# Phase copies with consecutive blocks for the key compression of a decoder step

## What is computed

```
def compress(k, pe, w1, w2):
    n_cmp = (k.shape[1] - CMP_BLOCK) // CMP_STRIDE + 1
    idx = jnp.arange(n_cmp)[:, None] * CMP_STRIDE + jnp.arange(CMP_BLOCK)[None, :]
    kb = k[:, idx] + pe[:, None, :]
    hid = jax.nn.silu(jnp.einsum("bclgd,ldh->bcgh", kb, w1))
    ...
    return jnp.einsum("bcgh,hd->bcgd", hid, w2), c_end
```

## Time and profile before

| | |
|---|---|
| median of three runs | 1095.35 us (1095.02 to 1096.1) |
| the profiled execution's own time | 1095.09 us |
| its span in the trace | 1092.9 us |
| PE busy | 1023.7 us, 94% of the span |
| DVE / ACT / POOL busy | 639.7 / 404.9 / 380.9 us |
| share of PE in the chain that ended last | 85% |
| first layer of the compression | from 588.62 to 665.22 us of the span |

### The profile page before, as it was taken

The page is one execution under the profiler, slowest core; times in us unless marked ns, Lnnn a source line. Parts: engine busy times, 40 slices in busy tenths (PEclk is TensorE's granted clock), DMA queues, the critical chain, the costliest instruction groups (busy, mean ns, idle before and its releaser), DMA issues.

```text
span 1092.9 us, 19375 instructions
## 1 busy us (share of the span) xinstructions
PE 1023.7 (94%) x7232; PEld 846.4 (77%) x7232; DVE 639.7 (59%) x1383; ACT 404.9 (37%) x794; POOL 380.9 (35%) x325
## 2 busy tenths in 40 slices
PE   2999999999999879998999999999789999999996
PEld 0989989989989568997997447999757777756685
DVE  5598998998998686214620001244688888844112
ACT  5333333333342584223311002135467777721001
POOL 2487887887887573010000000000323233200000
PEclk9999999999999879998999999999989999999797
DMA  8334533543541902340570004322260000260002
GB/s 330 94 102 110 169 110 101 155 134 98 137 154 40 317 12 82 109 162 1 198 189 1 1 0 147 112 78 78 78 241 1 0 1 1 96 232 1 1 1 82
DMA packets 43017, 108.02 MB, mean 99 GB/s; under 512 B 20675, under 2 KB 21731, under 8 KB 38531
## 3 DMA queue, kind: packets, MB, share of 16 engines
q1 hardware_dynamic: 42946, 106.99, 29.9%
HBM read 81.87 MB, written 12.17 MB: 86 GB/s over the span
## 4 chain that ended last, share of the span: by engine, by line
PE 85%; DVE 6%; ACT 3%; issue 3%; POOL 3%; DMA 0%; DVEq 0%; ACTq 0%
PE ps L561 49%; PE ps L944 7%; PE ps L721 5%; PE ps L834 5%; PE ps L587 4%; POOL C L1720 3%; PE ps L822 2%; PE ps L719 2%; PE ps L539 1%; PE ps L930 1%; PE ps L811 1%; PE ps L813 1%; DVE KL L1479 1%; PE ps L830 1%; PE ps L786 1%
## 5 line engine op out<-in xcount | busy, mean ns | idle before, releaser
L561 PE MATMUL ps<-Hh,ringAh 128*128 128x256 f32 (+1 forms) x768 | 161.0, 291 | 14.3 <-DVE X L1254 14.3
L561 PE MATMUL ps<-Hh,ringAl 128*128 128x256 f32 (+1 forms) x768 | 159.4, 289 | 0.0
L1298 DVE SCALAR_TENSOR_TENSOR acc<-VP,tapc,acc 128x512 f32<-128x512 f32 x122 | 159.2, 1305 | 0.0
L561 PE MATMUL ps<-Xl,ringAh 128*128 128x256 f32 (+1 forms) x768 | 158.1, 287 | 0.0
L1689 POOL TENSOR_TENSOR ringAl<-ringA,ringAh 128x1024 fp32r<-128x1024 f32 x48 | 121.3, 2541 | 73.2 <-ACT ringAh L1020 73.2
L561 PEld LDWEIGHTS ps<-Hh,ringAh 128*128 128x128 f32 x768 | 123.3, 189 | 27.2 <-DVE X L1254 14.6
L561 PEld LDWEIGHTS ps<-Xl,ringAh 128*128 128x128 f32 x768 | 123.9, 189 | 0.0
L561 PEld LDWEIGHTS ps<-Hh,ringAl 128*128 128x128 f32 x768 | 123.1, 189 | 0.0
L1298 DVE SCALAR_TENSOR_TENSOR ps<-VP,tapc,ps 128x512 f32<-128x512 f32 x138 | 102.8, 745 | 0.6
L834 PE MATMUL ps<-PTB,V 128*128 128x512 f32 (+3 forms) x256 | 91.0, 439 | 2.7 <-ACT PTB L1197 2.3
L561 PE MATMUL ps<-Hh,ringEh 128*128 128x256 f32 (+1 forms) x384 | 82.0, 295 | 7.0 <-DVE ringEl L1364 4.6
(11 more groups left out here) (232 smaller groups left out, 2086.7 us busy)
## 6 DMA issues: line engine op xcount, KB each, us to landing
ringA<-in_w_a SPq DMA_DIRECT2D x16, 1536.0 KB, 7.1
G<-VP SPq DMA_DIRECT2D x60, 260.0 KB, 4.8
ringE<-in_w_f SPq DMA_DIRECT2D x24, 512.0 KB, 3.3
ringC<-in_w_c SPq DMA_DIRECT2D x8, 1024.0 KB, 5.7
cache_cmp<-in_cache_cmp SPq DMA_DIRECT2D x32, 128.0 KB, 2.6
cache_sel<-in_cache_sel SPq DMA_DIRECT2D x16, 256.0 KB, 2.9
cache_win<-in_cache_win SPq DMA_DIRECT2D x1, 4096.0 KB, 13.6
out_win_s<-in_win_state SPq DMA_DIRECT2D x1, 4032.0 KB, 17.0
```

The lines of the kernel that those rows point to most:

```text
L561: mm = nc.tensor.matmul(dst, w, x[:, cols], start=begins, stop=ends)
L1298: nc.vector.scalar_tensor_tensor(tap_sum(k % 2), src, w, tap_sum(k % 2), ALU.mult, ALU.add).then_inc(conv_step, 1)
```

## The change

The key pairs are sorted by phase (pair index modulo 8) into copies on the chip, in which the blocks of one phase lie next to each other. As a block is 16 pairs and blocks are 8 pairs apart, pair 8a+m of block c (a is 0 or 1) is entry c+a of phase m. So PE reads columns a, a+1, a+2, ... of phase m.

- `KKm` [128, 2, 8 phases, 4*32+2] at NR: POOL fills it once, from `KK`, with one copy for each kv as soon as that kv's tiles are kept. Two columns at its end take the positional input of that phase for a=0 and a=1, so that the positional sum becomes column 128 of the same matmul. That matmul has 129 consecutive columns (32 for each group, of which 31 are used).
- `cmpm` [128, 8 phases, 32, 16] at G0: DVE fills it from `cache_cmp`, 16 copies of 128x512, each read with a step of 8 columns. It has room for one kv; the copies for kv=1 wait until PE is done with the same phase of kv=0 (`cmpm_used`). DVE starts after the last token tile (`tok_done` 5), since `wtokh` lies in the same bytes.
- PE issues two matmuls for each weight in place of three (129 columns of `KKm`, 480 columns of `cmpm` as 32 runs of 15), with the weights in the order m, a. It waits for `kkm_ready` once for each kv and for `cmpm_ready` ahead of each phase (16 waits).
- The memsets on POOL move: the pads of `hp` and `hs` lie in the bytes of `KKm`, so they are set after `hid_done` 2; the clearing of `vcd` and `qblk` stands behind them.
- ACT waits for `cmpm_used` 16 in place of `hid_done` 2; DVE's bias copy reads column 128 of banks 0 and 1.

```diff
@@ layout
+        KKm = at("KKm", [P, 2, CSUB, GROUPS * 32 + 2], NR)
+        cmpm = at("cmpm", [P, CSUB, SEQS * GROUPS, 16], G0)
@@ tensor
-            pe.wait_ge(cmp_in, 32 * SEQS * NPG)
             pe.wait_ge(v_kept, 4)
             for kv in range(2):
                 if kv == 1:
                     gate_rows()
-                for m in range(CBLK // 2):
-                    w, first, last = W1[:, kv, m, :], m == 0, m == CBLK // 2 - 1
-                    nc.tensor.matmul(ps[:, kv, 0:GROUPS * NCP], w, KK[:, kv, :, m:m + 8 * (NCP - 1) + 1:8],
-                                     start=first, stop=last)
-                    nc.tensor.matmul(ps[:, 4 + kv, 0:SEQS * GROUPS * NCS], w,
-                                     cache_cmp[:, kv, :, m:m + 8 * (NCS - 1) + 1:8], start=first, stop=last)
-                    mm = nc.tensor.matmul(ps[:, 6 + kv, 0:1], w, pe_in[:, kv, m:m + 1], start=first, stop=last)
-                mm.then_inc(hid_done, 1)
+                pe.wait_ge(kkm_ready, kv + 2)
+                for m in range(CSUB):
+                    pe.wait_ge(cmpm_ready, CSUB * kv + m + 1)
+                    for a in range(2):
+                        w, first, last = W1[:, kv, CSUB * a + m, :], m == a == 0, m == CSUB - 1 and a == 1
+                        mm = nc.tensor.matmul(ps[:, kv, 0:GROUPS * 32 + 1], w, KKm[:, kv, m, a:a + GROUPS * 32 + 1],
+                                              start=first, stop=last)
+                        if last:
+                            mm.then_inc(hid_done, 1)
+                        mm = nc.tensor.matmul(ps[:, 4 + kv, 0:SEQS * GROUPS * NCS], w, cmpm[:, m, :, a:a + NCS],
+                                              start=first, stop=last)
+                    mm.then_inc(cmpm_used, 1)
@@ scalar
-            act.wait_ge(hid_done, 2)
+            act.wait_ge(cmpm_used, 2 * CSUB)
@@ vector, ahead of the gate reduction
+            dve.wait_ge(cmp_in, 32 * SEQS * NPG)
+            dve.wait_ge(tok_done, 5)
+            for i in range(2 * CSUB):
+                kv, m = divmod(i, CSUB)
+                if kv:
+                    dve.wait_ge(cmpm_used, m + 1)
+                nc.vector.tensor_copy(cmpm[:, m], cache_cmp[:, kv, :, m::CSUB]).then_inc(cmpm_ready, 1)
...
-            nc.vector.tensor_copy(pe_hid[:], ps[:, 6:8, 0]).then_inc(pe_kept, 1)
+            nc.vector.tensor_copy(pe_hid[:], ps[:, 0:2, GROUPS * 32]).then_inc(pe_kept, 1)
@@ gpsimd
             pool.wait_ge(h2_ready, KT)
+            pool.wait_ge(small_in, 96)
+            nc.gpsimd.tensor_copy(KKm[:, :, :, GROUPS * 32:], pe_in[:].rearrange("p v (a m) -> p v m a", a=2)).then_inc(kkm_ready, 1)
+            for kv in range(2):
+                pool.wait_ge(kv_kept, 2 * kv + 2)
+                nc.gpsimd.tensor_copy(KKm[:, kv, :, 0:GROUPS * 32].rearrange("p m (g c) -> p m g c", g=GROUPS),
+                                      KK[:, kv].rearrange("p g (c m) -> p m g c", m=CSUB)).then_inc(kkm_ready, 1)
+            pool.wait_ge(hid_done, 2)
             nc.gpsimd.memset(hp[:, :, :, NCP:32], 0.0)
             nc.gpsimd.memset(hs[:].rearrange("p v g (s c) -> p (v g s) c", c=16)[:, :, NCS:16], 0.0).then_inc(pads2_set, 1)
```

More of the change, by code:

```diff
@@ L51 @@
 CSTRIDE, CBLK = 16, 32
+CSUB = CSTRIDE // 2
 NCP = (NP_ - CBLK) // CSTRIDE + 1
@@ L338, in build @@
         gates_ready = sem("gates_ready")
+        cmpm_ready = sem("cmpm_ready")
+        cmpm_used = sem("cmpm_used")
+        kkm_ready = sem("kkm_ready")
         hid_done = sem("hid_done")
@@ L1142, in _ @@
                 nc.scalar.activation(hp[:, kv, :, 0:NCP],
-                                     ps[:, kv, 0:GROUPS * NCP].rearrange("p (g c) -> p g c", g=GROUPS),
+                                     ps[:, kv, 0:GROUPS * 32].rearrange("p (g c) -> p g c", g=GROUPS)[:, :, 0:NCP],
                                      ACT.Silu, bias=pe_hid[:, kv:kv + 1]).then_inc(hid_ready, 1)
```

## The result

The changed kernel takes 0.966 of the time before (interval 0.962 to 0.971). Its four runs were 1056.9, 1058.1, 1066.0 and 1066.5 us (median 1062.05); those of the kernel before, beside it, 1095.0, 1095.4, 1096.1 and 1101.1 (median 1095.7). The profiled execution took 1058.09 us, with a span of 1056.0 against 1092.9. So 37 us are gained in the pair of profiles, where 41.2 were forecast, and the times of one kernel lie up to 10 us apart.

The account below looks back on a forecast made before the run. PE alone was taken to bound the compression stage; 0.96 first copy + 33.9 steps + 0.57 gate rows = 35.4 us against 76.6, so 1095.1 - 41.2 = 1053.9 us, range 1051.3 to 1061.5.

Parts of the forecast that it names:

- What bounds the kernel: Compression stage, 76.6 us: PE is busy throughout and no other engine shares in its end, so shortening it shortens the span.
- Cached keys: Compression stage, 32 matmuls of 480 columns in runs of 15: 0.82 us each, near the pace of consecutive columns, from 1.72.
- The 32 hops: Jumps between runs of 15 columns in each cached-keys matmul: possibly 0.06 us a matmul, 1.9 us in all, allowed in the range.
- New keys: Compression stage, 32 matmuls of 129 consecutive columns for 124 scattered ones: 0.24 us each, between 0.22 and 0.34.
- First copy: DVE's first copy of cached keys, on the path at the stage's start: 0.69 us plus 0.07 signal, PE starting 0.96 after 588.62.
- The worst bound of 1.45: Upper bound in us for DVE's first copy, if the 32-byte step slows DVE by PE's factor of 2.1.
- Other copies, waits, POOL's fill, moved memsets: DVE's other 15 copies, PE's 18 waits, POOL's KKm copies and later memsets: cost nothing; waits at most 0.9 us in all.
- The stage: Compression matmuls from 588.62 to the next tile: 35.4 us against 76.6, with 32 steps of 1.06 us; 41.2 less.
- The clock behind the stage: After the compression stage, dips of the clock can fall otherwise: put at 1 us either way in the range.
- a rival only for the compression stage: Whole compression stage at 1.2 GHz: steps of 2.12 us, time 1087.8; chance 0.02.
- The dip at 631: Grant fall near 631 us in the old compression stage, read as falling among slow matmuls; a dip as long costs about 2 us.
- Rival 3: Behind the stage, the gain is partly given back by a transfer now too late; a third of it gives 1068; chance 0.04.

## Why the prediction was right, and where it was off

- **What bounds the kernel, and that the stage's gain reaches what follows**: right. The stall behind it moved by 41.54 us, unchanged in length, and the first two bursts by 41.4.
- **Cached keys** at 0.82 us, measured 0.80 to 0.81: right, with its reason (a record is 566 ns, not 590). The 32 hops cost nothing (1.9 us had been allowed), and the run with other steps shows that it is the neighbour within 8 bytes that counts. One reading behind it was loose: of the matmul at 632.55 that was named as running at the lower level, only the first 0.8 us did, as the grant is back at 1.00 from 633.34. The one ahead of it lies in the low stretch whole (629.93 to 633.34), and bears the reading out with 1.71 us from start to start:

```profile
629.98 1.89 PE L721 MATMUL ps<-cache_cmp,W 128*128 128x480 f32 x2
631.69 0.40 PE L723 MATMUL ps<-pe_in,W 128*128 128x1 f32 x2
```

- **New keys** at 0.24, measured 0.22, the lower bound: mis-sized by 0.02, 0.6 us over the stage. It came out at 129/512 of the long matmul's time in rows 5, and not at that of the 128-column one.
- **First copy** at 0.96, measured 1.03; the copy was 0.62 and not 0.69, but the way from PE's end to DVE and back took 0.4. The worst bound of 1.45 didn't come. That DVE isn't slowed by the step does not follow: its consecutive move of 4352 columns takes 0.56 ns a column, the strided copies 1.05 (0.54 us for 512), and no consecutive copy of this shape was run.
- **Other copies, waits, POOL's fill, moved memsets** at nothing: right. PE waits nowhere else in the stage, and POOL's copies of 2.7 us lie 50 us and more ahead. POOL and DVE do get into each other's way, at no cost to the end: beside POOL's first copy (from 527.23) DVE's split takes 1.76 us, for 1.23, and beside the moved memsets its move of Hl takes 3.16, for 2.42:

```profile
529.28 1.76 DVE L1373 TENSOR_TENSOR ringEl<-ringE,ringEh 128x1024 fp32r<-128x1024 f32 x1 [1.46 <-ACT ringEh L1112]
```

- **The stage** at 35.4, measured 34.8; a step of the 32 came out at 1.03 us, not 1.06.
- **The clock behind the stage** is the term that failed. It stood there as "1 us either way", and as a rival only for the compression stage. It took 4.6 us in the profiled execution, which with the 0.3 us that the stage came out better (41.5 for 41.2) makes 1058.1 of 1053.9; the executions near 1066 lie 12 above the forecast. So two of the four runs lie above the range, and all four above the forecast. The range also isn't its own sum: 1 us on either side of 1052.6 and 1061.4 gives 1051.6 to 1062.4, not 1051.3 to 1061.5. The step that was wrong is "I know of nothing behind the stage that is timed from anything but PE": the clock is, and it was low for 3.4 us behind three of the four bursts. The dip at 631 was in hand as a sign, since the grant fell there with PE busy throughout, and it was read as a matter of slow matmuls alone. Rival 3, a gain given back in part behind the stage, came true in kind, with 4.6 of 41.5 us in place of a third, but had looked for a transfer.

## What to carry to other kernels

Lay out the moving operand so that each column has a neighbour within 8 bytes: here float32 matmuls took half the time for it. A copy on an idle engine cost only its first instalment, 1.03 us. A stretch in which PE runs nothing but short matmuls is a risk to what follows it even if PE is never idle; make it shorter with fewer and wider matmuls (this gave 8.6 us between the medians, of which some 3 are the shorter bursts themselves), not by scattering the short ones among long ones. Before crediting or blaming an edit for its last few microseconds, add a microsecond of idle work ahead of the fragile place: if the time moves by more than that, the clock may be in it. Then compare the granted clock over the whole span and not only at the edit, since what was won in the gate tiles was lost in the sample stage more than once.

## What the runs showed of the hardware that was not expected

- A float32 matmul of 480 columns takes 0.81 us with consecutive columns or runs of 15, 0.86 with columns 8 bytes apart, 1.71 with 16 and 1.72 with 32. With 32 bytes it takes 1.71 at 1.2 GHz as well (629.98 to 631.69, kernel before).
- DVE copied 128x512 float32 with a step of 32 bytes in 0.62 us, less than the 0.69 of an operation with two inputs; POOL's copy of 1024 columns with that step took 2.7 us and drew out DVE's split beside it from 1.23 to 1.76.
- The clock fell to 1.2 GHz for 3.4 us behind 2.43 us of short matmuls in which PE was busy throughout, or didn't, with the same instructions: in ten profiles 21 of 40 such bursts were followed by it. Behind 1.70 us of wider matmuls it never fell, in 8 of 8.
- PE's same instructions behind the gate tiles took 316 to 318 us, 321 to 322, or 324.6, by how long the sample stage was at the lower clock.
